# Three modulation tiles moved into the router's wait, and another slot order for the experts' weights

## What is computed

```
for l in range(2):
    mod = silu(c) @ w_ada[l] + b_ada[l]            # 6 x 1024 values: sh1, sc1, g1, sh2, sc2, g2
    h = modulate(rms_norm(x, norm1_g[l]), sh1, sc1)
    y = token_mixer(h, ...)                        # ... merged @ w_out
    x = x + g1 * y
    h = modulate(rms_norm(x, norm2_g[l]), sh2, sc2)
    y = hier_moe(h, ...)                           # router, then 2 of 32 experts for each token
    x = x + g2 * y
```

## Time and profile before

| what | value |
| --- | --- |
| three runs | 2197.21 us median (2196.18 to 2199.8) |
| profiled execution | 2198.59 us, span of its instructions 2196.8 us |
| busy share of PE, DVE, ACT, POOL | 94%, 45%, 32%, 13% |
| mean granted TensorE clock | 0.984 of full |
| read from HBM | 654.17 MB, 298 GB/s over the span |

### The profile page before, as it was taken

How to read it: one execution, slowest core, us unless ns; L and a number is a source line. 1 busy time by engine, 2 the same in 40 slices (tenths; PEclk the granted TensorE clock), 3 DMA queues, 4 the chain that set the end, 5 groups by cost and what they waited for, 6 DMA issues and landing times.

```text
span 2196.8 us, 29932 instructions
## 1 busy us (share of the span) xinstructions
PE 2071.8 (94%) x12687; PEld 1373.8 (63%) x12687; DVE 980.5 (45%) x1878; ACT 701.6 (32%) x1243; POOL 276.6 (13%) x141
## 2 busy tenths in 40 slices
PE   7999999999989999999999989899998999999999
PEld 4687784444434458877644443344764699978997
DVE  4466652222112137576322211111346587757776
ACT  3434431111101144453221110111213655566554
POOL 3554520000000035455000000000000000000000
PEclk9999999999999999999999999999999999999999
DMA  9966669999999997567799999999546285245550
GB/s 349 345 218 224 253 269 413 421 421 421 421 420 421 421 336 255 205 233 304 291 421 422 420 422 421 421 421 409 174 180 233 95 275 185 96 139 192 174 194 36
DMA packets 193589, 657.27 MB, mean 299 GB/s; under 512 B 12923, under 2 KB 116837, under 8 KB 131880
## 3 DMA queue, kind: packets, MB, share of 16 engines
q1 hardware_dynamic: 190784, 651.74, 76.2%
q0 software_dynamic: 1184, 2.08, 0.3%
q10 hardware_dynamic: 1480, 1.45, 0.2%
HBM read 654.17 MB, written 1.06 MB: 298 GB/s over the span
## 4 chain that ended last, share of the span: by engine, by line
PE 76%; DMA 16%; DVE 5%; ACT 1%; issue 1%; POOL 1%; SPq 1%; DVEq 0%; ACTq 0%; POOLq 0%
PE ps L410 74%; DMA ring<-in_w_expert_in 10%; DMA hT<-in_w_expert_in 1%; DMA XL<-in_w_expert_in 1%; DMA ring<-in_w_in 1%; DMA HB<-in_w_expert_out 1%; SPq L677 1%; DMA AR<-in_w_ada 1%; DVE AR L762 1%; PE ps L2144 1%; DVE ARr L1687 0%; DMA wr<-in_w_router_expert 0%; PE ps L2830 0%; PE ps L2652 0%; POOL cols L522 0%
## 5 line engine op out<-in xcount | busy, mean ns | idle before, releaser
L410 PE MATMUL ps<-ring,AR 128*64 128x512 f32 (+2 forms) x1952 | 536.2, 582 | 32.3 <-DMA ring<-in_w_expert_in 19.0
L410 PE MATMUL ps<-XLr,HBr 128*128 128x256 f32 x1280 | 369.6, 289 | 4.7 <-DVE XLr L1687 1.9
L410 PEld LDWEIGHTS ps<-ring,AR 128*64 128x64 f32 (+1 forms) x1952 | 184.4, 142 | 290.1 <-issue 238.3
L410 PE MATMUL ps<-hTr,ringr 128*128 128x256 f32 x1280 | 362.1, 283 | 0.0
L410 PE MATMUL ps<-hTr,HBr 128*128 128x256 f32 x1280 | 362.0, 283 | 0.0
L393 POOL TENSOR_TENSOR ringr<-ring,HBr 128x1024 fp32r<-128x1024 f32 x106 | 258.8, 2458 | 735.9 <-ACT HBr L387 735.7
L387 ACT ACTIVATE HBr<-ring 128x1024 fp32r<-128x1024 f32 x260 | 265.7, 1050 | 187.6 <-PE ps L410 159.9
L410 PEld LDWEIGHTS ps<-XLr,HBr 128*128 128x128 f32 x1280 | 245.3, 192 | 23.5 <-issue 15.1
L410 PEld LDWEIGHTS ps<-hTr,ringr 128*128 128x128 f32 x1280 | 245.4, 192 | 2.4 <-issue 1.4
L410 PEld LDWEIGHTS ps<-hTr,HBr 128*128 128x128 f32 x1280 | 245.3, 192 | 0.0
L393 DVE TENSOR_TENSOR ringr<-ring,HBr 128x1024 fp32r<-128x1024 f32 x154 | 183.9, 1223 | 82.8 <-ACT HBr L387 82.5
(11 more groups left out here) (325 smaller groups left out, 2784.2 us busy)
## 6 DMA issues: line engine op xcount, KB each, us to landing
ring<-in_w_expert_in SPq DMA_DIRECT2D x151, 1024.0 KB, 22.3
ring<-in_w_expert_out SPq DMA_DIRECT2D x77, 1024.0 KB, 20.8
ring<-in_mod_w SPq DMA_DIRECT2D x48, 1024.0 KB, 6.7
ring<-in_ffn_w_up SPq DMA_DIRECT2D x44, 1024.0 KB, 5.1
ring<-in_w_in SPq DMA_DIRECT2D x40, 1024.0 KB, 5.3
ring<-in_w_ada SPq DMA_DIRECT2D x40, 1024.0 KB, 7.1
HB<-in_w_expert_in SPq DMA_DIRECT2D x33, 1024.0 KB, 24.4
HB<-in_w_expert_out SPq DMA_DIRECT2D x23, 1024.0 KB, 19.1
```

The lines of the kernel that those rows point to most:

```text
L410: return pe.op.matmul(out_, lhsT, rhs, start=start, stop=stop, **kw)
```

## The change

Of the four tiles behind the groups of branch b only the one behind group 1 stays; the other three are multiplied in the router's wait, with one constant product behind them in place of five (layer 0) or three (layer 1). The row's copy on DVE moves behind `dve_low_tokens`, and its transposes and bias to the start of pair 1. The order of slots changes: in layer 0 from (8, 9, 10, 7, 5, 6, 1, 2, 3, 4, 0, 12, 13, 14), in layer 1 from (8, 9, 11, 6, 7, 5, 2, 3, 12, 13, 0, 1, 4). The wait for the last "o" product stands before slot 14 in layer 0 and 12 in layer 1. The loads themselves and their order do not change.

```diff
@@ pe_mixer
             for g in range(4):
                 pe_branch(pe, l, m, "b", g, (2, 3) if g < 2 else (0, 1, 2, 3))
-                pe_mods(pe, 1)
+                pe_mods(pe, 1 if g == 1 else 0)
...
                 else:
-                    pe_mods_turn(pe)
                     pe_router_shift(pe, l, moe[l])
@@ dve_mixer
-                dve_mods(dve, 1)
+                dve_mods(dve, 1 if g == 1 else 0)
             for k in (6, 7):
                 dve_half(dve, ("merged", l), m.dqkr, m.gmixr, m.gmix, k)
             dve_router_weights(dve, l, moe[l])
-            dve_mods_turn(dve)
@@ sp_moe
-            all_ = ((8, 9, 10, 7, 5, 6, 1, 2, 3, 4, 0, 12, 13, 14), (8, 9, 11, 6, 7, 5, 2, 3, 12, 13, 0, 1, 4))[l]
+            all_ = ((8, 9, 10, 1, 2, 3, 4, 0, 14, 7, 5, 6, 12, 13), (8, 9, 11, 2, 3, 12, 13, 0, 1, 4, 6, 7, 5))[l]
             sp.wait_ge(*pe_unit["branch", l, "b", 1, 1])
...
-                            if n_load == all_.index(12):
+                            if n_load == all_.index((14, 12)[l]):
                                 sp.wait_ge(*pe_unit["o", l, 3, 1])
@@ pe_router
             pe_stats(pe, l, m, 3)
-            pe_busy(pe, bank, 5 - 2 * l, "router", l)
+            pe_mods(pe, 3)
+            pe_busy(pe, bank, 1, "router", l)
@@ pe_moe_all
             for p in range(NE // 2):
+                if p == 1:
+                    pe_mods_turn(pe)
@@ dve_moe_all
             dve_low_tokens(dve, l, m)
+            dve_mods(dve, 3)
             for p in range(NE // 2):
+                if p == 1:
+                    dve_mods_turn(dve)
```

## The result

| | kernel before | changed kernel |
| --- | --- | --- |
| median of five runs | 2197.52 us (2196.18 to 2199.8) | 2209.03 us (2205.17 to 2213.6) |
| span of the profiled execution | 2196.8 | 2207.2 |
| share of TensorE's full clock | 0.984 | 0.981 |

The ratio is 1.005 with an interval of 1.0039 to 1.0062: slower by 11.5 us, where +6.4 was forecast; the time lies 0.5 us beyond the upper end of the range.

What follows compares the result with a forecast made beforehand. PE paces the kernel except in the expert phases, which the DMA stream bounds at 421 GB/s. Layer 0's +6.0 and layer 1's +0.4 make +6.4 us on the median 2197.21: 2203.6, range 2196 to 2208.5.

Steps and rivals of the forecast that it cites:

- Part 4: Experts' end: slot 0, now held by pair 15, makes the next mixer's weights late; +6.0 us layer 0, +0.4 layer 1.
- Part 1: Mixer's end: moving three tiles, the row's copy and the turn starts each layer's router 2.1 us earlier.
- the chain of halves: Mixer's end, ACT, POOL and DVE: 1.0 us earlier without the tile ahead of group 2, 1.6 without the copy.
- the hold by POOL: Mixer's end: POOL's instruction blocks DVE on the shared port; if it catches DVE once more, the gain is 0.
- Part 2: Router's wait: tiles replace constant products; no change in layer 0, +1.4 us in layer 1.
- Part 3: Weight stream through the router: no gap, so 2.1 us ahead in layer 0 and 0.3 ahead in layer 1.
- No gain at the mixers' end: Rival: POOL catches DVE's halves or half clock falls into DVE waits, losing the 2.1; +10.6, 2207.8 us, chance 0.15.
- its clock variant: Mixer's end: a half-clock stretch falls into the longer DVE waits, and the 2.1 us is gone.
- The clock does not fall: Rival, last scatter of layer 0: no half clock, or its fall hidden; the 2.1 goes, 2201.5 us, chance 0.20.
- the broken stream is mended: Rival, experts: loads fill the stream's pauses; -4.5, 2192.7 us, chance 0.15 shared with PE gaining 3.5 twice.

Runs made afterwards that it cites:

- experiment 1: Only the new order of slots, with the wait that goes with it, on the kernel before: 2205.88 us, ratio 1.0046.
- experiment 2: Changed kernel with slot 0 late in the ring, so load 178 holds it again in layer 0: 2200.25 us, ratio 1.0014.
- experiment 3: Changed kernel with ACT taking the last pair's down products out ahead of mixer 1's first two high halves: 2207.56 us, ratio 1.0045.
- experiment 7: Changed kernel with three constant products instead of one in layer 0's router: 2210.7 us, ratio 1.0056.
- experiment 4: Changed kernel with experiment 2's slot order, tiles kept behind groups 1 and 3 and two in the router: 2199.47 us, ratio 1.001.
- experiment 5: Kernel before with only the row's copy and turn moved late; tiles, constant products and slot order as before: 2195.22 us, ratio 0.9993.
- experiment 10: Changed kernel with two constant products ahead of each mixer's first o group: 2207.13 us, ratio 1.0033.
- experiment 8: Experiment 5's kernel with a fourth constant product in layer 1's router: 2197.53 us, ratio 0.9999.
- experiment 6: Experiment 5's kernel with two tiles behind group 2, one behind group 3, one replacing a router product, and another slot order: 2197.38 us, ratio 0.9996.
- experiment 9: Experiment 8's kernel with the tile behind group 0 replacing one router product, and experiment 6's slot order: 2195.97 us, ratio 0.9989.

## Why it came out so

**Part 4 was right,** in mechanism and size, and it is the main cause. For the order alone the prediction's terms are those of its rival: 6.0 and 2.1 of clock in layer 0, 1.8 and 0.7 in layer 1, 10.6 in all; experiment 1 gives +8.8. In its profile layer 0's experts are 8.1 longer, as forecast, and layer 1's 1.4 for 2.5. The issue, the landing, the scatter, PE's idle time and the half clock are all in the rows. The late loads took 5.3 (changed kernel) and 5.35 us (experiment 1) where the earlier trace rows had 5.2. The Trainium skill, "DMA: Bandwidth & Descriptors", on the anatomy of one DMA, has a fit for GpSimd's path that gives 4.4 by my estimate; for these loads on SP's queue the row decides. The price of lateness was read off a row of the old trace, that of the slot which load 189 held then.

**Part 1 failed, and it is the step that missed.** "I take 2.1" for each mixer's end became -0.2 to +1.1 of gain. What failed is not the chain of halves, which moved as worked out (1.6), nor the hold by POOL: the last pieces ran unhindered, 1.42 us for four, and the first again were held (2.95 for two). It is the clock. Taking tiles out from between the groups left PE 2.87 us of waits in place of 1.31, and the first o group ran at half from the second wait on. This is no accident of one execution: the profiles of the changed kernel and of experiments 2, 3 and 7 have the same code there, and none of their eight ends kept the clock; they took 55.08 to 55.96 us, where experiment 4's end at full clock took 53.57. The prediction had this in a subordinate clause of a rival ("or a half-clock stretch falls into the longer DVE waits"), at 0.15 and with no row; yet it priced the same effect at 2.1 in Part 4, from rows of the same trace. Experiments 4 (mixer 1) and 5 show the 2.1 and the 1.1 where the clock holds; 10 shows that filling the wait brings part of it back.

**Part 2 missed the same thing.** It set "three tiles for four products, 3.0 for 3.2". The row's 6.10 us for five products had a half-clock stretch in it; without it the new work takes 3.9, leaves PE waiting, and the gather pays 1.3. That the wait of 1.87 alone makes the gather slow is not shown: experiment 7 took it away and nothing was gained. Nor is the 1.3 a fixed price of the new code: experiment 2 had the stretch on the tiles and router 0 in 14.93. For layer 1 Part 2 forecast +1.4, and router 1 became 0.6 shorter.

**Part 3 held:** no gap between the routers and the experts, and no gain or loss that can be seen. In layer 1 the mixer's end gained 1.1 (2.1 forecast), the router 0.6 (a loss of 1.4 forecast), and the experts lost 2.1 (1.1 forecast). That the three add up to +0.3, for +0.4, is partly luck: two terms missed in opposite directions, and the experts, whose end the stream sets, took up most of the rest. The wait for the weights behind them was 0.76 for 0.7.

**The sum.** By the prediction's own terms the order alone costs 10.6, and the moved tiles and turns give back 4.2 (2.1 at each mixer's end). By medians the order costs 8.8 and the whole change 11.5, so the tiles and turns cost about 2.7 on top: 6.9 worse than forecast, of which an order cheaper by 1.8 hid a part; the miss is 5.1. In the two profiles, which differ by 10.4 us, it is 4.0. Mixer 0's end has 2.3 of that. Router 0 and layer 0's experts together have only 0.2 (8.3 for 8.1): the router's 1.3 came off again in the experts' stage, whose end hangs on the stream. The first stage has another 2.3, before any edited instruction ran, and the rest nearly cancels. These 2.3 us are there by 80 us (one and the same DVE instruction starts at 77.13 and at 79.46), and the clock was lower in that stretch (0.68 against 0.74 in 20 to 40). Whether that belongs to the kernel stays open: over the twelve profiles the first stage took 257.7 to 261.7 us, 259.8 or more in the five with three tiles moved, but 259.6 and 259.8 in experiments 8 and 6 as well.

**The rivals.** "No gain at the mixers' end", 2207.8, was the nearest: its sum of +10.6 stands against +11.5, and its clock variant is what happened in layer 0. "The clock does not fall" and "the broken stream is mended" are out.

## What to carry to other kernels

When a ring of buffers is reordered, look past its end: find who takes each slot next, and which load held it last; here one slot given up 26 us later cost 8 us in one layer. And useful work that fills a wait on TensorE is not free to move: what it leaves behind is idle time, and the products that follow can pay for it at half clock. Before counting on an end that is 2 us shorter, look at what the new waits add up to, and price the half clock from a stretch of the same trace; moving one filler (experiment 9, 2196.0) did better than moving three with slot 0 on time (experiment 2, 2200.3), and no better than moving none (experiment 5, 2195.2).

## What the hardware did that I had not expected

- A stretch at half clock came behind waits that are small one by one: 1.27 and 1.04 us, with products between them. The clock then was 0.57 over 8 us. Two waits of 1.04 and 1.02 us were followed by half clock in one mixer of experiment 4 and by full clock in the other.
- One or two products did not fill it away: in experiments 7, 8 and 10 the wait was filled or shortened, and a stretch at half came in the same gather (7, 8) or some 10 us later (10). The same code (layer 0 of kernels 5 and 8) had its gather once in 4.04 and once in 5.33 us.
- One float32 product of 128x512 took 1.22 us on average in a run of five that was about half at half clock and 0.94 at full (two in 1.88, experiment 10); a filler's length depends on the clock that it is meant to hold up.
